# Reordering the hand-over from the first phase to the experts: three weight loads, the context router and the second expert's tokens

## The reference, cut to what matters

```python
def _ec_moe(h, w_router, w_gate, w_up, w_down):
    Bn, T, _ = h.shape
    cap = EC_CAPACITY_FACTOR * T // N_EXPERTS
    probs = jax.nn.softmax((h @ w_router).astype(jnp.float32), axis=-1)
    gates, idx = lax.top_k(jnp.swapaxes(probs, 1, 2), cap)
    bidx = jnp.arange(Bn)[:, None, None]
    xs = h[bidx, idx]
    a = jax.nn.silu(jnp.einsum('becd,edf->becf', xs, w_gate)) * jnp.einsum('becd,edf->becf', xs, w_up)
    y = jnp.einsum('becf,efd->becd', a, w_down) * gates[..., None].astype(h.dtype)
    return jnp.zeros_like(h).at[bidx, idx].add(y)
...
    x = x + gate1 * m
    h = _rmsnorm(x, g_norm2) * (1.0 + scale2) + shift2
    x = x + gate2 * _ec_moe(h, w_router, w_gate, w_up, w_down)
```

## Time and profile before

| what | us |
|---|---|
| three runs | 853.18, 854.32 (median), 854.40 |
| the profiled execution's own time | 853.98 |
| its span, first to last instruction | 852.1 |
| PE busy | 830.2 |
| DVE busy | 502.6 |
| ACT busy | 233.3 |
| POOL busy | 60.6 |

### The profile page before, as it was taken

One profiled execution on the slowest core, in us unless ns is written; L12 is line 12 of the kernel. 1 busy time (PEld: TensorE's weight loads), 2 busy tenths in 40 slices (PEclk: granted clock), 3 DMA queues, 4 the chain that ended last, 5 costly groups with the idle time before them and its releaser, 6 DMA issues.

```text
span 852.1 us, 14545 instructions
## 1 busy us (share of the span) xinstructions
PE 830.2 (97%) x6034; PEld 455.7 (53%) x6034; DVE 502.6 (59%) x1233; ACT 233.3 (27%) x462; POOL 60.6 (7%) x74
## 2 busy tenths in 40 slices
PE   6999999999999999999999999999999999999995
PEld 5798899899897876333333333333333333333322
DVE  3676552869366568876556456456456465465436
ACT  5557543544243334020110110111011011011015
POOL 1000000000000002011011011011011011010033
PEclk9999999999999999999999999999999999999998
DMA  9955625352418939999999999999999999999993
GB/s 329 303 203 190 224 82 198 113 197 75 136 34 343 367 131 326 425 409 428 415 407 430 410 410 429 411 413 423 415 411 419 419 412 417 424 409 412 427 349 147
DMA packets 51014, 275.28 MB, mean 323 GB/s; under 512 B 5210, under 2 KB 14526, under 8 KB 38788
## 3 DMA queue, kind: packets, MB, share of 16 engines
q1 hardware_dynamic: 45484, 255.68, 74.3%
q0 software_dynamic: 3936, 13.77, 5.5%
q10 hardware_dynamic: 1528, 4.90, 1.5%
HBM read 260.83 MB, written 13.57 MB: 322 GB/s over the span
## 4 chain that ended last, share of the span: by engine, by line
PE 89%; DMA 3%; DVE 3%; ACT 2%; SPq 1%; issue 1%; POOLq 0%; DVEq 0%
PE pair L2466 26%; PE pair L2069 17%; PE pair L2445 12%; PE pair L2491 12%; PE pair L2306 7%; PE pair L2500 6%; PE pair L2009 2%; PE pair L2104 2%; DMA scale_b<-in_w_mod 2%; DMA xs<-hn,gather_idx 1%; PE pair L2227 1%; PE pair L2217 1%; PE pair L2018 1%; DVE aT L1847 1%; DMA out<-x_sb 0%
## 5 line engine op out<-in xcount | busy, mean ns | idle before, releaser
L2466 PE MATMUL pair<-ring,xT 128*64 128x512 f32 x1024 | 223.9, 594 | 1.4 <-ACT xT L1126 1.4
L2466 PEld LDWEIGHTS pair<-ring,xT 128*64 128x64 f32 x1024 | 72.1, 137 | 143.9 <-issue 141.7
L2491 PE MATMUL pair<-ring,aT 128*64 128x512 f32 x512 | 113.4, 595 | 0.6 <-DVE aT L1847 0.6
L2445 PE MATMUL pair<-ring,xT 128*32 128x512 f32 x1024 | 113.4, 594 | 0.0
L1126 ACT ACTIVATE xT<-xT,mod,scale 128x64 f32<-128x64 f32 x120 | 41.4, 427 | 218.9 <-DVE xT L1847 218.9
L1847 DVE STREAM_TRANSPOSE xT<-xs 32x256 f32<-32x256 f32 x180 | 78.3, 435 | 4.4 <-DMA xs<-hn,gather_idx 1.4
L1847 DVE STREAM_TRANSPOSE aT<-act_l 32x128 f32<-32x128 f32 x256 | 77.5, 303 | 4.1
L2491 PEld LDWEIGHTS pair<-ring,aT 128*64 128x64 f32 x512 | 35.8, 137 | 76.8 <-issue 76.8
L2069 PE MATMUL pair<-hT_hi,w_hi 128*128 128x320 f32 x320 | 76.0, 319 | 0.0
L2445 PEld LDWEIGHTS pair<-ring,xT 128*32 128x32 f32 x1024 | 31.5, 110 | 79.4 <-issue 79.4
L2069 PE MATMUL pair<-hT_lo,w_hi 128*128 128x320 f32 x320 | 73.1, 310 | 0.0
(11 more groups left out here) (332 smaller groups left out, 940.6 us busy)
## 6 DMA issues: line engine op xcount, KB each, us to landing
ring<-in_w_up SPq DMA_DIRECT2D x32, 2048.0 KB, 29.0
ring<-in_w_down SPq DMA_DIRECT2D x32, 2048.0 KB, 19.7
ring<-in_w_gate SPq DMA_DIRECT2D x31, 2048.0 KB, 24.9
p1w<-in_w_mod SPq DMA_DIRECT2D x8, 2048.0 KB, 7.9
p1w<-in_w_in SPq DMA_DIRECT2D x5, 2048.0 KB, 7.9
p1w<-in_w_mod SPq DMA_DIRECT2D x7, 1024.0 KB, 11.8
x_sb<-in_x_sample SPq DMA_DIRECT2D x8, 512.0 KB, 5.8
p1w<-in_w_out SPq DMA_DIRECT2D x2, 2048.0 KB, 8.7
```

Of the source, the lines that this page charges most:

```text
L2445: ins = mm(ctx_ps[32 * g:32 * g + 32, :], xt[:, 4 * half + j, CAP_L:96], w[:, j, n * 512:(n + 1) * 512], start=half == 0 and j == 0, stop= ...
L2466: ins = mm(ps[64 * n:64 * n + 64, :], xt[:, kk, 0:CAP_L], w[:, j, n * 512:(n + 1) * 512], start=kk == 0, stop=kk == KC - 1)
L2491: ins = mm(y_ps[0][r:r + 64, :], aT[:, j, 64 * fh:64 * fh + 64], wd[:, j, n * 512:(n + 1) * 512], start=fh == 0 and j == 0, stop=fh == 1 a ...
```

## The change

Four regroupings; no instruction is added or removed but waits.

- SP: loads 4 and 5 both wait for `wo4` and for the landing of the first gather (`xs_full[0]`); load 9 waits for the landing of the second (`xs_full[1]`).
- PE: the gathered rows of expert 0 are turned ahead of tile 4's turn; `router(4)` goes into expert 0 ahead of chunk 1, `router_sum(4)` between gate and up of chunk 1; `ctx_probs` from chunk 2 to chunk 3, `choose_first_ctx` from chunk 4 to chunk 5.
- ACT: the first two token chunks of expert 0 ahead of tile 4's copy and its sum of squares, the other six behind.
- DVE: `ctx_parts` behind the fourth round; in expert 0, `tokens(1)` ahead of `choice` and of the wait for the second gate row.

```diff
@@ -593,10 +593,10 @@
             for j in range(3):
                 load_part(BY_ROWS, j)
             sp.wait_ge(wo_half, NT)
+            sp.wait_ge(job_done, job("wo4") + 1)
+            sp.wait_ge(xs_full[0], 16)
             load_rows(4)
-            sp.wait_ge(job_done, job("wo4") + 1)
             load_rows(5)
-            sp.wait_ge(xs_full[0], 16)
             sp.wait_ge(ctx_scaled, 1)
             sp.dma_start(hn[tile(NT - 1), :], xr[:, 0, :]).then_inc(hn_out[0], 16)
             load_rows(6)
@@ -605,6 +605,7 @@
             load_part(BY_ROWS, 3)
             sp.wait_ge(job_done, job("lg4") + 1)
             sp.wait_ge(sums_ctx, 32)
+            sp.wait_ge(xs_full[1], 16)
             load_rows(9)
             for n in range(TURNS, 6 * (E - 1)):
                 load_later(n)
@@ -1111,9 +1112,9 @@
 
             second_gate(0)
 
-            def first_tokens():
-
-                for kk in range(KC):
+            def first_tokens(lo, hi):
+
+                for kk in range(lo, hi):
                     act.wait_ge(xTp_done, kk // 4 + 1)
                     ins = a.activation(xT[:, 0, kk, 0:CAP_L], xT_ps(kk)[:, 0:CAP_L], ACT.Identity,
                                        bias=mod[:, 3 * KC + kk, 0:1], scale=scale2[:, kk, 0:1])
@@ -1181,10 +1182,11 @@
                     last_square(1)
                     last_sqrt(1)
 
+            first_tokens(0, 2)
             h2_turn(NT - 1)
             act.wait_ge(x2c_ready, 2)
             square_sum(NT - 1)
-            first_tokens()
+            first_tokens(2, KC)
             act.wait_ge(smax_ready, 2)
             a.activation(probs[:, NT - 1, :], probs[:, NT - 1, :], ACT.Exp).then_inc(exp_ready, 1)
             act.dma_start(sum_c[0:P, :], x_sb[:, NT - 1, :]).then_inc(sums_ctx, 16)
@@ -1801,8 +1803,8 @@
             v.memset(xT[:, 0, :, SLOTS:96], 0.0).then_inc(pads_zero, 1)
             rounds(2, 3)
             high_chunks(NT - 1)
+            rounds(3, 4)
             ctx_parts()
-            rounds(3, 4)
             ctx_normal()
             router_row(NT - 1)
             softmax(NT - 1, NT, 2)
@@ -1893,9 +1895,9 @@
                     ins = turned(aTc, act_c, s, 4)
                 ins.then_inc(aTc_ready, 1)
                 if k == 0:
+                    tokens(e + 1, k + 1)
                     choice()
                     dve.wait_ge(g2_ready, 2)
-                    tokens(e + 1, k + 1)
                 if k == E - 1:
                     dve.wait_ge(froot_ready, 1)
                     inverse_after(rms, slice(0, 3), rms[:, 0, 0:3], finv_ready)
@@ -2456,11 +2458,15 @@
                     for j in range(4):
                         kk = 4 * half + j
                         if k == 0:
-                            if kk == 4:
+                            if kk == 1:
+                                router(4)
+                            if kk == 5:
                                 choose_first_ctx()
                             pe.wait_ge(*((xT_first, kk + 1) if kk < KC - 1 else (xT_lat, 1)))
                         for ps, w in ((gate_ps, wg), (up_ps, wu)):
-                            if k == 0 and kk == 2 and w is wu:
+                            if k == 0 and kk == 1 and w is wu:
+                                router_sum(4)
+                            if k == 0 and kk == 3 and w is wu:
                                 ctx_probs()
                             for n in range(2):
                                 ins = mm(ps[64 * n:64 * n + 64, :], xt[:, kk, 0:CAP_L], w[:, j, n * 512:(n + 1) * 512],
@@ -2502,8 +2508,6 @@
                                      stop=fh == 1 and j == 3)
                     ins.then_inc(d_used, 1)
 
-            turn_tile(4)
-            router(4)
             pe.wait_ge(pads_zero, 1)
             pe.wait_ge(xs_full[0], 16)
             claim_last(pe, 2)
@@ -2511,7 +2515,7 @@
                 ins = turn(xT_ps(kk)[:, 0:CAP_L], xs[0:CAP_L, 0, tile(kk)], ident[0:CAP_L, 0:CAP_L])
                 if kk % 4 == 3:
                     ins.then_inc(xTp_done, 1)
-            router_sum(4)
+            turn_tile(4)
             claim_last(pe, 0)
             for e in range(E):
                 expert(e, e)
```

## The result

The changed kernel takes 861.18 us (median of 6 runs, 860.86 to 862.46) where the kernel before takes 854.04 (6 runs, 853.18 to 855.55): ratio 1.0085, interval 1.0073 to 1.0097. It is **slower by 7.1 us**, outside the range. The profiled execution took 861.27 us, span 859.4 against 852.1. Its first phase happened to run 0.85 us earlier (first gather issued at 322.76 against 323.61; over all profiles here that issue lies between 322.2 and 323.8, whatever the edit).

The account below looks back on a forecast made before the run. TensorE sets the time, with weight transfers close behind. A stream 5.2 us late less 3.7 us of lead gives +1.5, PE's 0.8 gain being used up in waiting: 853.98 + 1.5 = 855.5 us, range 853.0 to 858.0.

Parts of the forecast that it names:

- PE's front: PE's work around experts 0 to 2: PE alone would gain 0.8 us (-0.1 to 1.4).
- Router wait: Before the context router's products: PE's wait of 0.93 us for the copy of tile 4 goes.
- the index: In expert 0: the last index comes at 347.7 instead of 346.99, and PE's turn of the indices waits 0.3 us.
- aT stall: In expert 1, after the later gather of expert 2: PE stalls 0.6 us for aT, between none and 1.5.
- The gather of expert 2: POOL's gather waits for choice and moves from 360.35 to 366.8; it takes 10.7 us and lands at 377.5.
- That is 2.4 later: Weight loads after the first gather: load 7 lands at 352.2 instead of 349.8, 2.4 us later.
- I take the middle, 4.7: Second gather, ahead of load 9: takes 4.7 us, between 2.8 bare and 6.6 beside a load; 2.8 us of stream lost.
- rival 1: Slower: second gather takes 6.6 us beside loads 7 and 8, stream 7.0 late, end 857.3; chance 0.30.
- 5.2 - 3.7 = +1.5 at expert 14: At expert 14: a stream 5.2 us late, less 3.7 us of lead, moves the end by +1.5 us.
- lead of 3.7: Expert 14: the second half of w_up lands at 780.7, 3.7 us before PE begins its second half at 784.4.
- The tail hangs on PE ... have some 5 us: Tail: the final rows' loads come 5 us later but have some 5 us before ScalarE's last scaling needs them.
- same: The outcome of a time within 0.2% (1.7 us) of the kernel before; chance 0.50.

Follow-up runs that it names:

- loads 4 and 5 alone: The kernel before, with loads 4 and 5 both moved behind the first gather and no other edit: 857.4 us, ratio 1.0047.
- final rows on ACT's queue: The changed kernel with the five final row loads issued by ACT on its own queue instead of by SP: 860.9 us, ratio 1.0091.
- two products on DVE: The changed kernel with the final products of tiles 3 and 1 done by DVE instead of POOL, each in one operation with its scaling: 860.24 us, ratio 1.0071.
- order alone: The new order on PE, ACT and DVE, with SP's whole program that of the kernel before: 860.25 us, ratio 1.0079.
- after, load 9 free: The changed kernel with one wait taken out, so load 9 no longer waits for the second gather: 858.2 us, ratio 1.0058.
- before, rows late: The kernel before, with SP loading the final rows only when the last down weights have landed: 855.86 us, ratio 1.0023.

## Why the prediction was wrong

**PE's front: right, step by step.** Router wait gone, expert 0 at 329.9 aligned (330.0 forecast), 0.33 for the index (0.3), 0.43 in front of expert 1 (0.6) at 365.88, aligned 366.7 (366.5); aT stall 1.0 (0.6, in its bounds). The first gather landed 3.9 us after its issue, at the upper end of the forecast (326.5 to 327.5; 327.5 aligned). The gather of expert 2 went out at 366.27, aligned 367.1, and took 11.2 (366.8 and 10.7).

**"That is 2.4 later": it was 5.2 (aligned), and 5 in the run with loads 4 and 5 alone.** The step laid the whole work behind 328.5 end to end at 416 GB/s. In after the engines moved 109 GB/s in the three microseconds of the gather and of the new start (share 0.52, above), and 389 GB/s on the mean from 328 to 354. Those 26 us at 389 instead of 416 are an estimated 1.7 of the 2.8 us that were missed; the rest is not traced.

**"I take the middle, 4.7": the second gather took 7.0,** a little more than rival 1's 6.6. Its time goes with what stands around it and not with its size: 4.5 with load 7 landed before its issue, 7.0 with load 7 at 354.2 and the quarter load at 356.5, 12.3 with load 9 behind it. So the first error feeds the second. Behind it comes the second restart, 246 and 98 GB/s from 357 to 359. By the Trainium skill (DMA: Bandwidth & Descriptors, Anatomy of one DMA) the gather would take an estimated 2.75 us; no gather of 80 rows here came near it, the shortest taking 4.5.

**"5.2 - 3.7 = +1.5 at expert 14": the subtraction holds, its first number does not, and the stop came in expert 11.** With 7.9 it gives 4.2 of PE time; PE is 4.8 late (aligned). So the lead of 3.7 was sized well. The loss showed mainly as one stop of 2.49 us and a stretch at the lower clock behind it, 8.78 - 7.09 = 1.7 us more:

```profile
692.00:694.00 2.00, 1.95 (x8) 0.87 (x10) 0.00 (x0) 0.00 (x0) 0.00 (x0) 0.83 1.02 346
694.00:696.00 2.00, 2.00 (x7) 0.64 (x5) 0.00 (x0) 0.00 (x0) 0.00 (x0) 0.50 1.03 422
```

The lower clock does not set the total, though. In two runs with the same SP waits (final rows on ACT's queue; two products on DVE) the stops in expert 11 were 2.48 and 2.49 and the clock did not fall:

```profile
693.26 7.09 PE L2472 MATMUL pair<-ring,xT 128*64 128x512 f32 x32 [2.48 <-DMA ring<-in_w_up]
756.94 7.09 PE L2472 MATMUL pair<-ring,xT 128*64 128x512 f32 x32 [0.39 <-DMA ring<-in_w_up]
789.08 7.09 PE L2472 MATMUL pair<-ring,xT 128*64 128x512 f32 x32 [0.42 <-DMA ring<-in_w_up]
```

PE then waited for ring loads again in experts 13 and 14 and reached the last down products 4.6 and 5.1 us late (aligned), where after has 4.8. What the lower clock takes there, the later loads would have taken for the most part.

Why expert 11: the prediction looked at the last lead alone. In before the second half of w_up of expert 11 lands at 683.9, 5.9 us ahead of PE (689.8); in after it lands at 691.9, 8.8 later aligned, so 2.9 are missing there, where expert 14 misses 4.2. These halves land 32.1 to 32.7 us apart in most experts, but in before 32.9 and 32.8 apart into experts 10 and 11, and in after 32.1 and 34.2. Why the stream loses time there in both kernels stays open.

**"The tail hangs on PE ... have some 5 us": this step failed outright,** priced 0, measured 3.3. It asked when ACT needs the rows and not who else works on them. POOL's 9.4 us of products begin when they land, and DVE's operations with two inputs in SBUF stand still until the running product is over. In all sixteen profiles in which a 128x3 operation of DVE is blocked, its end is the end of a POOL product to 0.03 us. The tail is longer by about what POOL's end overhangs the start of DVE's first such operation, less 0.2 to 0.4:

| profile | POOL ends | DVE begins | overhang | wait of PE for left_l |
|---|---|---|---|---|
| before | 836.36 | 836.54 | -0.2 | none |
| order alone | 844.85 | 844.84 | 0.0 | none |
| after, load 9 free | 840.22 | 838.62 | 1.6 | 1.4 |
| before, rows late | 837.46 | 835.08 | 2.4 | 2.2 |
| after | 844.17 | 840.62 | 3.6 | 3.2 |

The Trainium skill, SBUF — State Buffer, section SBUF: two separate sides, says that DVE and GpSimd share a port pair as an exclusive lock, held for a whole instruction, and that a DVE operation with two SBUF inputs needs it against a GpSimd operation that reads SBUF. Every row here agrees.

What counts is when the rows land against PE. POOL's first product begins 4.1 us before PE's last down products in before, 1.9 before them with load 9 free, 1.2 before them with the rows late, and 0.1 behind them in after; from those products to the end it takes 21.4, 22.8, 23.6 and 24.7 us. Beyond some 0.8 us of slack, where 5 were claimed, a late row costs one for one.

The sum with measured terms: PE 4.8 late at the last down products (4.2 of it by stream against lead), plus 3.3 in the tail, less the 0.85 by which the first phase ran early, gives the 7.3 us of span. Rival 1 had the mechanism of the late gather and nearly its time, but priced neither the first stretch at its 5.2 nor the tail; its 7.0 us of lateness and 857.3 came nearest. The direction, slower, was among the cases at 0.42; "same" was favoured for want of these two terms. What stays open: why the stream loses time in front of experts 10 and 11, and whether a version exists that keeps the 1 us gained in front and beats the kernel before.

## What to carry to other kernels

A hole cut into a saturated queue costs the hole, the restart (two microseconds at 246 and 98 GB/s here) and the backlog that later small transfers meet. Follow that lateness to every consumer, the ones in the middle of the series too, and to the transfers behind the last weights. In a tail, compare when each helper engine ends with when the next begins, to a tenth of a microsecond: GpSimd's long products and VectorE's short two-input operations exclude each other. Price a stop of TensorE of two microseconds or more at its length and, as a chance, 1.5 to 1.8 us more at the lower clock; where loads that land just in time set the pace behind it, as here, most of that extra does not reach the end.

## What the runs showed of the hardware

- A two-input DVE operation of 0.16 us shows as up to 2.4 us of busy time while POOL multiplies (1.22, 2.30, 2.41); the profile shows no wait there, only a long mean. One-input operations (RECIPROCAL, 0.18) and those with their large input in PSUM (0.75) kept their time.
- Nine stops of PE between 2.13 and 3.75 us ahead of the tail (2.49 in after) were followed by a stretch at a granted clock of 0.5; two of 2.48 and 2.49, in the runs with the final rows on ACT's queue and with two products on DVE, were not. Single stops of 0.9 to 1.6 were not followed by it. Two close together went either way: 0.93 and 0.88 were (the first 20 products of expert 0 took 7.11 us instead of 4.51, in the kernel before with its final rows on ACT's queue), 0.93 and 1.14 were not (before with load 6 early and load 10 waiting). So no rule by the length of a stop alone comes out of these runs.
- An indirect gather of 80 rows took 4.5, 7.0, 11.2, 11.6 and 12.3 us, the shortest with no 2 MB load ahead of it, the longest with a load queued right behind it.
